# Block inverse in a two-model kernel: the level-0 factor written by VectorE instead of multiplied by the identity

## The reference

```python
decay = jnp.exp(jnp.where(incl, gcum[..., :, None] - gcum[..., None, :], -jnp.inf))
m = jnp.where(strict, jnp.einsum('nbhik,nbhjk->nbhij', k_beta, k) * decay, 0.0)
eye = jnp.eye(CHUNK, dtype=m.dtype)
t_inv = lax.linalg.triangular_solve(eye + m, jnp.broadcast_to(eye, m.shape), left_side=True, lower=True)
u = jnp.einsum('nbhij,nbhjv->nbhiv', t_inv, v * beta[..., None])
w = jnp.einsum('nbhij,nbhjk->nbhik', t_inv, k_beta * jnp.exp(gcum)[..., None])
```

## Time and profile before

| | before |
|---|---|
| median of 3 runs | 1488.94 us (1488.91 to 1489.6) |
| profiled execution | 1487.75 us, its span 1485.9 us |
| TensorE matmul busy | 1471.3 us, 99% of the span |
| VectorE / ScalarE / GpSimd busy | 951.0 / 819.0 / 214.2 us |
| granted TensorE clock, mean | 0.998 |

### The profile page before, as it was taken

How to read it: one execution, slowest core, us unless ns; L and a number is a source line. 1 busy time by engine, 2 the same in 40 slices (tenths; PEclk the granted TensorE clock), 3 DMA queues, 4 the chain that set the end, 5 groups by cost and what they waited for, 6 DMA issues and landing times.

```text
span 1485.9 us, 27073 instructions
## 1 busy us (share of the span) xinstructions
PE 1471.3 (99%) x11622; PEld 1369.5 (92%) x11622; DVE 951.0 (64%) x1393; ACT 819.0 (55%) x1268; POOL 214.2 (14%) x125
## 2 busy tenths in 40 slices
PE   9999999999999999999999999999999999999998
PEld 8999899989998889998899989998889999899997
DVE  6655476686655475655557685655477777667756
ACT  6554376655544365544476654554465675555752
POOL 0000142113000260000331140000430001400001
PEclk9999999999999999999999999999999999999999
DMA  9655464237555456555553156555455334553341
GB/s 382 239 198 188 157 223 143 93 111 261 183 195 195 170 219 213 189 186 193 196 178 139 58 196 220 195 199 191 177 213 197 116 141 158 208 191 141 126 159 57
DMA packets 40086, 267.28 MB, mean 180 GB/s; under 512 B 4448, under 2 KB 4960, under 8 KB 9760
## 3 DMA queue, kind: packets, MB, share of 16 engines
q1 hardware_dynamic: 38160, 259.87, 49.2%
q0 software_dynamic: 944, 4.38, 0.7%
q10 hardware_dynamic: 864, 1.31, 0.2%
HBM read 264.49 MB, written 1.05 MB: 179 GB/s over the span
## 4 chain that ended last, share of the span: by engine, by line
PE 97%; DVE 2%; DMA 0%; ACT 0%; issue 0%; SPq 0%
PE PS L586 19%; PE PS L588 19%; PE PS L587 19%; PE PS L581 6%; PE PS L583 6%; PE PS L582 6%; PE PS L622 4%; PE PS L619 4%; PE PS L620 4%; PE PS L657 1%; PE PS L1239 1%; PE PS L963 1%; PE PS L1257 1%; PE PS L1249 1%; PE PS L1268 1%; PE PS L1277 0%
## 5 line engine op out<-in xcount | busy, mean ns | idle before, releaser
L586 PE MATMUL PS<-xTH,WH 128*128 128x256 f32 x2256 | 637.7, 283 | 0.0
L588 PE MATMUL PS<-xTH,rawL 128*128 128x256 f32 x2256 | 624.4, 277 | 0.0
L587 PE MATMUL PS<-xTL,WH 128*128 128x256 f32 x2256 | 624.4, 277 | 0.0
L1965 DVE TENSOR_TENSOR rawL<-raw,WH 128x1024 fp32r<-128x1024 f32 (+1 forms) x408 | 495.2, 1240 | 112.3 <-ACT WH L1398 111.8
L1398 ACT ACTIVATE WH<-raw 128x1024 fp32r<-128x1024 f32 (+2 forms) x477 | 484.0, 1045 | 128.5 <-PE PS L622 99.9
L586 PEld LDWEIGHTS PS<-xTH,WH 128*128 128x128 f32 x2256 | 423.8, 188 | 8.3 <-issue 5.6
L587 PEld LDWEIGHTS PS<-xTL,WH 128*128 128x128 f32 x2256 | 424.0, 188 | 2.7 <-issue 1.9
L588 PEld LDWEIGHTS PS<-xTH,rawL 128*128 128x128 f32 x2256 | 424.1, 188 | 0.0
L2658 POOL TENSOR_TENSOR rawL<-raw,WH 128x1024 fp32r<-128x1024 f32 (+2 forms) x70 | 165.1, 2387 | 767.3 <-ACT WH L1398 767.3
L1478 ACT ACTIVATE sg<-PS 128x256 f32<-128x256 f32 x79 | 30.3, 384 | 169.2 <-PE PS L588 169.2
L2084 DVE TENSOR_TENSOR hh<-PS,sg 128x256 f32<-128x256 f32 x79 | 33.5, 424 | 137.1 <-ACT sg L1478 137.1
(11 more groups left out here) (408 smaller groups left out, 2033.8 us busy)
## 6 DMA issues: line engine op xcount, KB each, us to landing
raw<-in_weights SPq DMA_DIRECT2D x233, 1024.0 KB, 4.8
gb<-in_lngb SPq DMA_DIRECT2D x16, 512.0 KB, 5.3
raw<-in_weights SPq DMA_DIRECT2D x2, 1056.0 KB, 4.7
gb<-in_ln SPq DMA_DIRECT2D x4, 512.0 KB, 4.6
cst<-in_consts POOLq DMA_DIRECT2D x1, 1378.5 KB, 10.2
raw<-in_weights SPq DMA_DIRECT2D x4, 256.0 KB, 5.3
x0T<-in_xT ACTq DMA_DIRECT2D x4, 256.0 KB, 5.7
xt<-in_x POOLq DMA_DIRECT2D x1, 1024.0 KB, 17.5
```

The source lines that it names most:

```text
L586: e.matmul(out, u.H(i, c0, 128), xH, start=first, stop=False)
L587: e.matmul(out, u.H(i, c0, 128), xL, start=False, stop=False)
L588: return e.matmul(out, u.L(i, c0, 128), xH, start=False, stop=end)
L1965: e.tensor_tensor(u.L(i, 0, w), u.R(i, w), u.H(i, 0, w).bitcast(F32), ALU.subtract).then_inc(*low_dve.up(k))
```

## The change

VectorE forms level 0 itself, in `T` in place of `U`: identity minus `Bs[0]`, untransposed. To have the blocks lie where the transpose of 128x128 needs them, each half of the rows is written to either half of `T`'s rows ("its flipped place"), which takes four instructions over 64 rows. TensorE transposes `T` (four transposes), and ScalarE copies the result into `U`. Level 1 has no transposes of its own, since `T` is there already, and waits for that copy instead. GpSimd's mask of level 2, which overwrites `Bs[0]`, waits for VectorE's writes in place of the product.

```diff
@@ TensorE
-            eye8 = C("eye64").unsqueeze(1).to_broadcast([128, 8, 64])
-            b = B(("level0", l), 5, (inverse_updated, (l, 0, 1)))
+            def flip(n, M, b):
+                B(("flip", l, n), b, (inverse_copied, (l, n, "flip")))
+                for g in range(4):
+                    ins = e.transpose(PS[:, b, 128 * g:128 * g + 128], M[:, 2 * g:2 * g + 2, :].rearrange("p i s -> p (i s)"), ident)
+                ins.then_inc(*inverse_product.up((l, n, "flip")))
             e.wait_ge(*gram_masked.at((l, "level0")))
-            for i in range(8):
-                for a in range(2):
-                    R = slice(64 * a, 64 * a + 64)
-                    ins = e.matmul(PS[R, b, 64 * i:64 * i + 64], Bs[0][R, i, :], eye8[R, i, :], start=True, stop=True)
-            ins.then_inc(*inverse_product.up((l, 0, "U")))
+            flip(0, T, 6)
             quarter("z", 0, 3)
             quarter("z", 1, 0)
...
             for n, (fb, zbanks, ub, q1, q2) in levels.items():
-                b = B(("flip", l, n), fb, (inverse_copied, (l, n, "T")))
-                e.wait_ge(*inverse_updated.at((l, n - 1, 1)))
-                for g in range(4):
-                    ins = e.transpose(PS[:, b, 128 * g:128 * g + 128], U[:, 2 * g:2 * g + 2, :].rearrange("p i s -> p (i s)"), ident)
-                ins.then_inc(*inverse_product.up((l, n, "T")))
+                if n == 1:
+                    e.wait_ge(*inverse_copied.at((l, 0, "flip")))
+                else:
+                    e.wait_ge(*inverse_updated.at((l, n - 1, 1)))
+                    flip(n, U, fb)
@@ ScalarE
             z_out(0)
             rounds("z", 1, 0)
             for n in range(1, 6):
-                e.wait_ge(*inverse_product.at((l, n, "T")))
-                e.activation(m.T[:, :, :], PS[:, bank["flip", l, n], :].rearrange("p (i s) -> p i s", i=8), ACT.Copy).then_inc(
-                    *inverse_copied.up((l, n, "T")))
+                f = 0 if n == 1 else n
+                e.wait_ge(*inverse_product.at((l, f, "flip")))
+                e.activation((m.T if f else m.U)[:, :, :], PS[:, bank["flip", l, f], :].rearrange("p (i s) -> p i s", i=8), ACT.Copy).then_inc(
+                    *inverse_copied.up((l, f, "flip")))
@@ VectorE
-            e.tensor_tensor(m.Bs[0][:, :, :], Es[:, :, :], C("lev0").unsqueeze(1).to_broadcast([128, 8, 64]), ALU.mult).then_inc(
-                *gram_masked.up((l, "level0")))
-
+            link(e.tensor_tensor(m.Bs[0][:, :, :], Es[:, :, :], C("lev0").unsqueeze(1).to_broadcast([128, 8, 64]), ALU.mult))
+            linked()
+            eye = C("eye64").unsqueeze(1).to_broadcast([128, 4, 64])
+            for a in range(2):
+                for i in range(2):
+                    R, Ro = slice(64 * a, 64 * a + 64), slice(64 * i, 64 * i + 64)
+                    ins = e.tensor_tensor(m.T[Ro, a:8:2, :], eye[R, :, :], m.Bs[0][R, i:8:2, :], ALU.subtract)
+            ins.then_inc(*gram_masked.up((l, "level0")))
             lows("z", 0, 2)
-            eye = C("eye64").unsqueeze(1).to_broadcast([128, 4, 64])
-            e.wait_ge(*inverse_product.at((l, 0, "U")))
-            for t in range(2):
-                v = PS[:, bank["level0", l], 256 * t:256 * t + 256].rearrange("p (i s) -> p i s", i=4)
-                e.tensor_tensor(U[:, 4 * t:4 * t + 4, :], eye, v, ALU.subtract).then_inc(*inverse_updated.up((l, 0, t)))
@@ GpSimd
                 if n > 1:
-                    e.wait_ge(*inverse_product.at((l, n - 2, "Z" if n > 2 else "U")))
+                    e.wait_ge(*(inverse_product.at((l, n - 2, "Z")) if n > 2 else gram_masked.at((l, "level0"))))
```

More of the change, by code:

```diff
@@ L964, in quadrants @@
                 return ins
-            eye8 = C("eye64").unsqueeze(1).to_broadcast([128, 8, 64])
-            b = B(("level0", l), 5, (inverse_updated, (l, 0, 1)))
-            e.wait_ge(*gram_masked.at((l, "level0")))
-            for i in range(8):
-                for a in range(2):
-                    R = slice(64 * a, 64 * a + 64)
-                    ins = e.matmul(PS[R, b, 64 * i:64 * i + 64], Bs[0][R, i, :], eye8[R, i, :], start=True, stop=True)
-            ins.then_inc(*inverse_product.up((l, 0, "U")))
+            def flip(n, M, b):
[3 more added lines that the diff above has]
+                ins.then_inc(*inverse_product.up((l, n, "flip")))
+            e.wait_ge(*gram_masked.at((l, "level0")))
+            flip(0, T, 6)
             quarter("z", 0, 3)
             quarter("z", 1, 0)
-            levels = {1: (6, (5, 7), (4, 6), ("z", 1, 1), ("z", 1, 2)), 2: (5, (7, 4), (6, 5), ("z", 1, 3), ("sb", 0, 0)),
+            levels = {1: (None, (5, 7), (4, 6), ("z", 1, 1), ("z", 1, 2)), 2: (5, (7, 4), (6, 5), ("z", 1, 3), ("sb", 0, 0)),
                       3: (4, (6, 5), (7, 4), ("sb", 0, 1), ("sb", 0, 2)), 4: (5, (7, 4), (6, 5), ("sb", 0, 3), ("sb", 1, 0)),
```

## The result

| | before | after |
|---|---|---|
| median (8 runs each) | 1489.27 us (1488.3 to 1489.99) | 1494.11 us (1491.38 to 1496.49) |
| ratio, 95% interval | | 1.0032 [1.0023, 1.0042] |
| profiled execution, its span | 1487.75, 1485.9 us | 1495.94, 1493.9 us |
| TensorE matmuls in the page | 11622 | 11558 |

The account below looks back on a forecast made before the run. The prediction took TensorE, busy for 99% of the span, to bound the kernel. Per layer -1.34 + 1.45 + 2.20 = +2.31 us, for two layers +4.6, so 1488.94 becomes 1493.5 us, range 1491.2 to 1495.2.

Parts of the forecast that it names:

- The saved work: TensorE at the block inverse: level-0 product and level 1's transposes removed, four lone transposes added; 1.34 us less per layer.
- The first wait: TensorE's transposes of T wait for VectorE's four writes at level 0; 1.45 us per layer.
- The hold-up by GpSimd: GpSimd's level-1 mask stalls VectorE's first write, making the first wait 1.45 us; without it 0.48 us, a rival of chance 0.10.
- the handover: Time from another engine's end to TensorE's start, taken as 0.13 us.
- The second wait: TensorE's first product of level 1 waits for ScalarE's copy into U, behind z_out(0) and a rounding; 2.20 us per layer.
- The sum: Saved work and both waits together: 2.31 us more per layer, 4.6 us more for two layers.
- The third rival, the clock: TensorE's clock falls; two quarters behind the second wait run at 1.2 GHz, 5.5 us more in all, about 1499; chance 0.05.
- the clock stays at 1.00: Sign expected in the changed profile: TensorE's granted clock does not drop from 1.00.
- The likeliest case: Both waits at the block inverse as worked out, giving 1492.7 to 1494.4 us; chance 0.80.

Follow-up runs that it names:

- e6: The kernel before without the level-0 product: VectorE writes identity minus Bs[0] straight into U, not transposed; ratio 0.9989.
- e2: The changed kernel with GpSimd's mask of level 1 started only behind VectorE's four writes; ratio 1.0026 to the kernel before.
- e4: The changed kernel with ScalarE's copy into U ahead of z_out(0) and the four transposes moved behind quarter z,0,3; ratio 0.9998 to the kernel before.
- e1: The changed kernel with ScalarE's copy into U moved ahead of z_out(0) and the rounding behind it; ratio 0.9999 to the kernel before.
- e8: The changed kernel with ScalarE's copy into U placed between z_out(0) (its Silu) and the rounding; ratio 1.0019 to the kernel before.
- e5: The kernel before with one more wait: TensorE's first product of level 1 waits for ScalarE's copy of the level's transposes; ratio 1.002.
- after_again_c: The changed kernel profiled again with no edit, one of three such executions, which took 1493.79, 1495.62 and 1495.94 us.
- e3: The changed kernel with both the copy into U ahead of z_out(0) and GpSimd's level-1 mask behind the four writes; ratio 0.9986 to the kernel before.
- e9: The changed kernel with Silu in z_out(0) done four times over with the same result, lengthening the second wait; ratio 1.0085 to the kernel before.

## Why the prediction was right

The median, 1494.11 us, is 0.6 over the 1493.5 predicted and in the range; the direction and both waits were as worked out. By its steps, per layer, measured without a fall of the clock:

- The saved work, -1.34: the product measured 1.22 in place of 1.29 (e6). Four transposes alone cost 250.53 - 249.91 - 0.11 = 0.51 (0.50). What is left over when the two waits are taken from the stretch is 2.15 - 1.35 - 2.11 = -1.31. The size is right; its other terms were not measured one by one.
- The first wait, +1.45: measured 1.35. The hold-up by GpSimd, which decided between 0.48 and 1.45, is shown by e2. The Trainium skill, "SBUF — State Buffer", section "Who interferes with whom", lets the one that issues first hold the other up; the traces agree in both directions, with the first write at 1.395 us behind GpSimd's mask and that mask at 2.33 us behind L1968 in e2. The 0.10 too much is mostly the handover: I took 0.13 us from ScalarE's copy of `Z`, and TensorE started 249.91 - 249.86 = 0.05 behind the last write. The 0.13 belongs to that place: where the product waits for the copy of `Z`, in e4, it starts 0.14 us behind it.
- The second wait, +2.20: measured 2.11, again by a handover of 255.34 - 255.29 = 0.05. That ScalarE's order makes it is shown by e1 and e8, which take away all of it or the rounding's part.
- The sum, +2.31: measured +2.15, so 4.3 us for two layers by the waits alone.
- The third rival, the clock, had a chance of 0.05 and is the step that I mis-sized; of the signs that the prediction names, only "the clock stays at 1.00" did not come. It fell in 4 of the 8 profiled passes. How often it falls over many executions stays open: three of the eight timed ones have a mean clock of 0.999, the highest that before shows, though one fall takes about 0.001 off it. Its price was mis-sized too: 1.5 us per fall in place of 2.73, since only one quarter and the product behind it, not two quarters, run at 1.2 GHz. The likeliest case and this rival are not alternatives but hold together: 4.3 us from the waits in every execution, and 0, 1.5 or 3.0 more. From before's median that gives 1493.6 to 1496.6, to which comes the scatter of single executions that before has too; the runs of after reach from 1491.4 to 1496.5.
- That the median came within 0.6 us is in part luck. The sum had the waits and the saved work together 0.3 us too high for two layers, and the clock at nothing. With falls in half of the passes it would be 4.3 + 1.5 = 5.8 us, about 1495.1, close to the range's upper end; the measured difference is 4.8, and its interval, 3.4 to 6.3 us, holds both.

What misled me on the clock were two rows of one execution: a wait of 2.6 us in the list, and a clock of 1.00 behind one of 1.4 us. The first place is at 1096 us, and the clock is indeed 1.00 behind it in the profile of before. But it is a draw: the same wait of 2.64 or 2.65 us has a lowered clock behind it in six of the thirteen profiles of this study (e1, e4, e5, e6, e8 and after_again_c), and not in the other seven, before, e3 and the first of after among them. Before, then e1, behind that wait:

```profile
1098.00:1100.00 2.00, 2.00 (x12) 1.69 (x11) 2.00 (x3) 1.73 (x3) 0.00 (x0) 1.00 0.91 268
```

```profile
1098.00:1100.00 2.00, 2.00 (x7) 1.51 (x7) 1.82 (x2) 1.06 (x2) 0.00 (x0) 0.50 0.67 250
```

No edit touches this place, so the kernel before very likely pays for such falls too in some executions, though its one profile shows none there. What makes a wait of 2.0 to 2.6 us lower the clock in one execution and not in the next stays open: in the profiles here waits of 1.1 to 1.6 us in the inverse never did (e1, e5, e8), and 3.9 us did in both layers (e9).

The Trainium skill, "TensorE: Matmul & The Clock Gate", Part 1, has the clock fall after idle time. The falls here agree, each behind a wait of 2.0 us or more; the four passes of after without one show that a wait as long need not bring it.

## What to carry to other kernels

Work moved off the engine that bounds the kernel pays only if its replacement is ready in time, and the replacement's place in the other engine's order counts as much as its length: here 0.6 us of copying behind a table load and a rounding cost 2.1 us, and ahead of them nothing (e1). Count the cover (what the bounding engine has to do meanwhile) against the whole chain ahead of the handover, and again for what the moved instruction pushes back, as e4 shows. And read a clock of 1.00 in one profiled execution as one draw: where a change makes TensorE stand as long as here, 2 us or more, price the fall of the clock as something that happens part of the time.

## What was not expected of the hardware

- With the same program and waits of the same length to within 0.03 us, the granted clock fell behind the 2.0 us wait in 4 of 8 passes, each fall costing 1.5 us; behind an old wait of 2.64 us it fell in 6 of 13 profiles.
- VectorE instructions over 64 of the 128 rows with 256 elements follow each other at 0.44 us, whether they cross to the other half of the rows or not (1.74 us for four that stay, 1.72 for four of which two cross). In both places each one reads or writes another half than the one ahead of it; no row here has several in a row on one half.
- A GpSimd instruction of 1.30 us took 2.33 when VectorE's subtraction with two inputs in SBUF had started 0.05 us ahead of it (e2).
